# Matmul order in the wide products: all high-weight products of a slab first, then all low-weight ones

## The chip, the cores and the metric

The kernel runs on one core of a Trainium2 chip. The metric is the device time of one execution in microseconds (us), the median over runs. Lower is better.

## The reference

The reference is two blocks over 256 tokens of width 1024. The first is a gated mixer followed by a feed-forward of retrieved single-neuron experts, the second is two layers with two SwiGLU feed-forwards and an attention mixer each. What matters here are the feed-forwards:

```python
# first block: 16384 experts, 8 heads of 16 chosen ones per token
act = jax.nn.gelu(jnp.einsum('thkd,td->thk', expert_u[ib], hb), approximate=False)
return jnp.einsum('thk,thkd->td', gb * act, expert_v[ib])
...
# second block, four times, D_FF = 2816
def swiglu(h, w_gate, w_up, w_down):
    return (jax.nn.silu(h @ w_gate) * (h @ w_up)) @ w_down
```

The kernel computes the expert feed-forward densely: all 16384 experts for all tokens, with a matrix G of gates that is zero where an expert was not chosen. Everything is float32.

## The kernel before

**Slabs.** All weights come from one stream in HBM, cut into slabs of 128 by 1024 numbers (512 KB). A ring of four buffers (`RING = 4`) holds them: `raw` as it landed, `w_hi` (ACT casts it, line 714) and `w_lo` (DVE subtracts `w_hi` from `raw`, line 1192). Both parts are of the type fp32r. The activations are split in the same way into `h_hi` and `h_lo`, which lie side by side in `h_parts`. A product of two float32 numbers is thus taken as high times high, plus high weight times low activation, plus low weight times high activation. The product of the two low parts is left out.

**Two ways of multiplying a slab.** A slab is eight k-tiles of 128 rows (`KT = 8`) that are summed in one PSUM region. `three` (line 1989) issues three matmuls of 256 columns for each k-tile. `wide` (line 2011) issues two: the high weights against high and low activations at once (512 columns, a whole PSUM bank: high products in the left half, low ones in the right half), and then the low weights against the high activations (256 columns, added to the left half). The two halves are added later by ACT (lines 772 and 774) and DVE (lines 1276 and 1283).

**The loops.** `mlp` (line 2103) is the PE program of a feed-forward. For each step it calls `feed`, which multiplies the step's one slab (experts, `fronts_ == 1`) or two slabs (SwiGLU: gate and up, `fronts_ == 2`) into the tile `front`, and then `drain` of the step before, which multiplies the third slab with the hidden values of that step into the tile `acc`. In the expert loop `drain` is twelve matmuls of 512 columns, in the SwiGLU loops twenty-four of 256. The expert loop has 108 steps with a `feed` (20 more steps come with a `drain` alone, after them), each SwiGLU has 22 steps. `feed` uses `wide` for all 108 slabs of the expert loop, and in each SwiGLU from step 2 on for all slabs but the very last (39 slabs of 44).

**What orders the work.** Each engine has a program written out by hand, and semaphores between them. PE waits for `lo_ready` once ahead of a slab (`wait_slab`), and counts `slab_used` up once, on the last matmul of a slab. ACT and DVE take `front` after that count, and ACT may overwrite `w_hi` of that ring buffer after it. SP loads the next slab into a ring buffer when `lo_ready` says that `raw` was split.

Of the kernel before, what the change touches and what calls it, by code (L numbers as in the profile page):

```python
# [28 lines left out]
P = 128  # L29
T = 256  # L30
D = 1024
KT = D // P
# [15 lines left out]
RING = 4  # L48
# [144 lines left out]
def build(nc, stream, x_in, cols_in, ones_in, keys_in, wpool_in, mixc_in, attc_in, out):  # L193
# [5 lines left out]
    at = 0  # L199
# [51 lines left out]
    with ExitStack() as ctx:  # L251
# [7 lines left out]
        w_hi = sb("w_hi", W_HI, [RING, D], F32R)  # L259
        w_lo = sb("w_lo", W_LO, [RING, D], F32R)  # L260
        h_parts = sb("h_parts", H_HI, [2, KT, T], F32R)
        assert H_LO == H_HI + KT * T
        h_hi, h_lo = h_parts[:, 0, :, :], h_parts[:, 1, :, :]
# [116 lines left out]
        fronts = front[:, :, :]  # L380
# [1601 lines left out]
        def _(pe):  # L1982
            def mm(out, lhsT, rhs, start, stop, **kw):
                return nc.tensor.matmul(out, lhsT, rhs, start=start, stop=stop, **kw)  # L1984
# [23 lines left out]
                    r = readers[j - before]  # L2008
                    pe.wait_ge(tile_read[r], reads(r, j - before))

            def wide(bank, slot, k):

                c = k * P
                mm(bank, w_hi[:, slot, c:c + P], h_parts[:, :, k, :], k == 0, False, skip_group_check=True)
                return mm(bank[:, 0:T], w_lo[:, slot, c:c + P], h_hi[:, k, :], False, k == KT - 1,
                          skip_group_check=True)

            def project(name, i, n, hi, lo, lows=None, ks=range(KT), parts={}, sum_of=None):

# [83 lines left out]
            def mlp(n0, steps, fronts_, done, seeded, banks_done, q=None, more=0, late_sum=False):  # L2103
                per_step = fronts_ + 1

                def wait(turn, turns, sm, v):
                    if turn is None:
                        pe.wait_ge(sm, v)
                    else:
                        pe.wait_ge(sm, turn * turns + v)  # L2110

                def feed(s, n, turn=None, turns=0, sum_of=None):
                    S0 = done + s
                    whole = fronts_ == 1 or s >= 2
                    if s >= 2 or turn is not None:

                        wait(turn, turns, scaled_ready, S0 - 1 if fronts_ == 1 else S0)
                    if q is not None and s == 0:
                        first_two([fronts[:, 0, f * T:(f + 1) * T] for f in range(2)], n, q, True)
                        return  # L2120
                    for f in range(fronts_):
                        wait_slab(n + f, turn, turns * per_step)
                        at = f if whole and fronts_ == 2 else s % 2
                        alone = f == 1 and s == steps - 1 and turn is None
                        for k in range(KT):
                            if whole and not alone:
                                ins = wide(fronts[:, at, :], (n + f) % RING, k)
                                continue
                            ins = three(fronts[:, at, f * T:(f + 1) * T], (n + f) % RING, k * P,
                                        h_hi[:, k, :], h_lo[:, k, :], k == 0, k == KT - 1)  # L2130
                            if sum_of is not None and f == 0 and k == 3:
                                norm(sum_of)
                        ins.then_inc(slab_used, 1)

                def drain(s, n, turn=None, turns=0, last=False):

                    S0 = done + s
                    wait(turn, turns, mid_lo_ready, S0 + 1)
                    wait_slab(n, turn, turns * per_step)
                    begin = s == 0 and not seeded and turn is None  # L2140
                    for b in range(4 if seeded else 0):

                        a, c = [part[:, s % 2, b // 2 * P:(b // 2 + 1) * P] for part in (mid_hi, mid_lo)]
                        hi, lo = [part[:, n % RING, b % 2 * D // 2:(b % 2 + 1) * D // 2] for part in (w_hi, w_lo)]
                        mm(banks[:, b, :], a, hi, False, False, skip_group_check=True)
                        mm(banks[:, b, :], c, hi, False, False, skip_group_check=True)
                        ins = mm(banks[:, b, :], a, lo, False, False, skip_group_check=True)
                        if last:
                            ins.then_inc(bank_done, 1)
                    for m in range(0 if seeded else KT):  # L2150

                        ins = three(acc[:, m, :], n % RING, m * P, mid_hi[:, s % 2, :], mid_lo[:, s % 2, :],
                                    begin and m % 2 == 0, False, skip_group_check=True)
                        if last and m % 2:

                            ins.then_inc(bank_done, 1)
                    if not last:
                        ins.then_inc(slab_used, 1)
                    else:
                        pe.wait_ge(bank_done, banks_done + 4)  # L2160
                        pe.sem_inc(slab_used, 1)

                feed(0, n0)
                n = n0 + fronts_
                turns = 4 if fronts_ == 2 else 2

                if q is not None and not late_sum:
                    norm(q)
                feed(1, n, sum_of=q if late_sum else None)
                if q == 2:  # L2170

                    for tt in range(TT):
                        pe.wait_ge(token_diag_ready, tt + 1)
                        ins = mm(tile[:, 2, tt * P:(tt + 1) * P], ones, final_diag[:, tt, :], True, True)
                    ins.then_inc(token_spread, 1)
                drain(0, n + fronts_)
                n += per_step
                loops = (steps - 2 - (fronts_ == 2)) // turns
                with pe.Fori(0, loops) as turn:
                    for c in range(turns):  # L2180
                        feed(2 + c, n + c * per_step, turn, turns)
                        drain(1 + c, n + c * per_step + fronts_, turn, turns)
                for s in range(2 + loops * turns, steps):
                    m = n + (s - 2) * per_step
                    feed(s, m)
                    drain(s - 1, m + fronts_)
                for s in range(steps - 1, steps + more):
                    drain(s, n0 + steps * per_step - 1 + (s - steps + 1), last=s == steps + more - 1)
# [42 lines left out]
            n = first["w_in"]  # L2231
            for i in range(44):
                if i in (MIX_V, MIX_V + 2):
                    project_tokens("w_in", i, i - MIX_V, n + i, h_hi, h_lo)
                elif i < PLAIN:
                    free_tile(i)
                    pe.wait_ge(landed[i], 16)
                    for k in range(KT):
                        if i == 0:
                            pe.wait_ge(h0_by["dve" if k & 2 else "act"], k // 4 * 2 + k % 2 + 1)  # L2240
                        ins = mm(tile_buf(i), raw[:, i, k * P:(k + 1) * P], h0[:, k, :], k == 0, k == KT - 1)
# [9 lines left out]
                if i == FIRST_LEVEL + 18:  # L2251
# [3 lines left out]
                    for pair in range(HEADS // 2):  # L2255
                        ins = outputs(vv, pair, fr[:, pair, :],
                                      lambda h: (S[:, h % 2, h // 2, :], S_off[:, h % 2, h // 2, :],
                                                 S[:, 2 + h % 2, h // 2, :]))
                    ins.then_inc(o_done, 1)
                if i == FIRST_LEVEL + 20:  # L2260
                    pe.wait_ge(o_sq, 1)
                    pe.wait_ge(mixc_landed, 16)
                    for b in range(2):
                        ins = mm(banks[:, b, :], head_ones,
                                 osq[:, 2 * b:2 * b + 2, :].rearrange("p a t -> p (a t)"), True, True)
# [3 lines left out]
            n = first["branch"]  # L2269
            for m in range(8):  # L2270
# [3 lines left out]
                for half in range(2):  # L2274
                    for k in range(4):
                        kk_ = 4 * half + k
                        ins = three(tile_buf(j, half), (n + m) % RING, kk_ * P, y_hi[:, kk_, :],
                                    y_lo[:, kk_, :], k == 0, k == 3)
                ins.then_inc(slab_used, 1)
            n = first["w_out"]  # L2280
            for m in range(8):
                project("w_out", m, n + m, h_hi, h_lo)
            if "peer" in first:
# [29 lines left out]
                n = first["wquery"]  # L2313
# [27 lines left out]
                for a in range(TOPK):  # L2341
                    pe.wait_ge(chosen_ready, a + 1)
                    for side in range(2):
                        for tt in range(TT):
                            ins = mm(tile[:, side, tt * P:(tt + 1) * P],
                                     chosen[:, a % 8, (side * TT + tt) * HEADS:(side * TT + tt + 1) * HEADS, :]
                                     .rearrange("p h k -> p (h k)"), ident_16[:, :],
                                     a == 0 and side == 0 and tt == 0, a == TOPK - 1, skip_group_check=True)
                    ins.then_inc(chosen_used, 1)
                    if a == GATES_AT:  # L2350
                        pe.wait_ge(picks_ready, 1)
                        for tt in range(TT):
                            ins = nc.tensor.transpose(tile[:, 2, tt * P:(tt + 1) * P],
                                                      gts[:, tt, :, :].rearrange("p h k -> p (h k)"), ident)
# [31 lines left out]
                for tt in range(TT):  # L2386
                    pe.wait_ge(x_tokens_by_act, tt + 1)
                    for k in range(KT):
                        if k == KT // 2:
                            pe.wait_ge(x_tokens_by_dve, tt + 1)  # L2390
                            pe.wait_ge(token_squares, 1)
                        ins = nc.tensor.transpose(turned_x(k)[:, tt * P:(tt + 1) * P],
                                                  x_tokens[:, tt, k * P:(k + 1) * P], eye[:, :])
# [5 lines left out]
            for kind, i in layer_stages():  # L2399
# [5 lines left out]
                elif kind == "even":  # L2405
# [36 lines left out]
                    n = first["even_in"]  # L2442
# [21 lines left out]
                    for g in range(2):  # L2464
                        pe.wait_ge(stick_e, g + 1)
                        for pair in (2 * g, 2 * g + 1):
                            ins = outputs(av, pair, fr[:, pair, :],
                                          lambda h: [az[:, h, c * P:(c + 1) * P] for c in range(3)])
                        ins.then_inc(ao_done, 1)
                    n = first["even_out"]  # L2470
# [4 lines left out]
                else:  # L2475
# [40 lines left out]
                    n = first["qkv"]  # L2516
# [119 lines left out]
```

## Time and profile before

| | |
|---|---|
| median of 3 runs | 2080.64 us (2077.79 to 2083.43) |
| the profiled execution | 2078.67 us, its span 2076.9 us |
| PE matmul busy | 2021.4 us, 97% of the span, 13232 matmuls |
| PE weight loads busy | 1822.9 us, 88% |
| DVE busy | 1511.5 us, 73% |
| ACT busy | 1126.5 us, 54% |
| DMA | 353.71 MB, mean 170 GB/s |
| mean granted TensorE clock | 0.996 |
| chain that ended last | PE 88%, DVE 7%, ACT 3% |

The expert loop lies between 423 and 1085 us of the span, the four SwiGLU feed-forwards after it. Matmuls are pipelined: the time that the profile gives for one matmul is longer than the distance from its start to the start of the next, so durations of matmuls can't be added up. What can be added up are distances between starts, and the pieces of the chain that ended last.

### The profile page before, as it was taken

The numbers are of one execution on the slowest core, as the hardware profiler recorded it, in microseconds if no ns is written. First come the engines' busy times: TensorE is split into PE (matmuls) and PEld (weight loads), VectorE is DVE, ScalarE is ACT, GpSimd is POOL, SyncE is SP. The second block draws the span as 40 slices with busy tenths as digits, with TensorE's granted clock in tenths as the row PEclk, the third lists the DMA queues.
The fourth block names the chain that finished last, engine by engine and source line by source line (L and its number), as shares of the span: only waits on it lengthen the run. The fifth ranks groups of instructions, "written<-read, shape, count | busy, mean of one in ns | idle before, by whom it ended". The sixth has DMA issues, their size and how long they took to land.

```text
span 2076.9 us, 37250 instructions
## 1 busy us (share of the span) xinstructions
PE 2021.4 (97%) x13232; PEld 1822.9 (88%) x13232; DVE 1511.5 (73%) x2563; ACT 1126.5 (54%) x1834; POOL 59.8 (3%) x40
## 2 busy tenths in 40 slices
PE   7999899999999999999999999999999999999998
PEld 7999888978888888888888999899999999999998
DVE  5868898867777777777777667666667667957665
ACT  5444528855555555555555555645555555645554
POOL 0000530000000000000000000000000000000000
PEclk9999999999999999999999999999999999999999
DMA  6346542146556555555664555445555555535553
GB/s 216 127 135 214 181 130 82 44 162 187 187 184 190 191 182 190 188 188 185 205 228 164 185 188 167 137 158 182 182 183 183 182 182 183 163 123 173 186 187 112
DMA packets 101464, 353.71 MB, mean 170 GB/s; under 512 B 11392, under 2 KB 16640, under 8 KB 101120
## 3 DMA queue, kind: packets, MB, share of 16 engines
q1 hardware_dynamic: 100944, 350.13, 52.0%
q10 hardware_dynamic: 432, 2.36, 0.3%
q8 instruction: 61, 1.00, 0.2%
q14 instruction: 27, 0.22, 0.0%
HBM read 348.77 MB, written 3.67 MB: 170 GB/s over the span
## 4 chain that ended last, share of the span: by engine, by line
PE 88%; DVE 7%; ACT 3%; issue 1%; DMA 0%; SPq 0%; DVEq 0%; ACTq 0%
PE front L1984 39%; PE acc L1984 33%; PE tile L1984 15%; DVE w_lo L1192 1%; ACT w_hi L714 1%; DVE chosen L1709 0%; DVE cand L1652 0%; ACT G L962 0%; PE front L2501 0%; DMA raw<-stream 0%; DVE x L1372 0%; ACT picks_raw L956 0%; ACT picks_mid L956 0%; DVE rstd L1214 0%; ACT h_parts L740 0%
## 5 line engine op out<-in xcount | busy, mean ns | idle before, releaser
L1984 PE MATMUL front<-h_parts,w_hi 128*128 128x512 f32 (+1 forms) x2432 | 813.7, 384 | 5.0 <-ACT h_parts L740 2.1
L1192 DVE TENSOR_TENSOR w_lo<-raw,w_hi 128x1024 fp32r<-128x1024 f32 x612 | 748.4, 1223 | 90.5 <-ACT w_hi L714 90.0
L714 ACT CAST w_hi<-raw 128x1024 fp32r<-128x1024 f32 x628 | 656.2, 1046 | 143.4 <-PE tile L1984 67.4
L1984 PE MATMUL front<-h_parts,w_lo 128*128 128x256 f32 x2272 | 636.2, 281 | 0.0
L1984 PEld LDWEIGHTS front<-h_parts,w_hi 128*128 128x128 f32 x2432 | 448.0, 189 | 100.3 <-issue 3.9
L1984 PEld LDWEIGHTS front<-h_parts,w_lo 128*128 128x128 f32 x2272 | 430.2, 189 | 4.1
L1984 PE MATMUL tile<-h_parts,w_hi 128*128 128x256 f32 x1344 | 248.0, 286 | 5.7 <-DVE w_lo L1192 2.6
L1276 DVE TENSOR_TENSOR scaled<-front,scaled 128x512 f32<-128x512 f32 x76 | 52.6, 692 | 228.4 <-ACT scaled L774 228.4
L1984 PEld LDWEIGHTS tile<-h_parts,w_hi 128*128 128x128 f32 x1344 | 209.3, 192 | 8.9 <-issue 6.9
L1984 PE MATMUL acc<-w_hi,mid_hi 128*128 128x512 f32 x512 | 203.1, 397 | 3.4 <-DVE mid_lo L1300 3.4
L1984 PE MATMUL acc<-mid_hi,w_hi 128*128 128x256 f32 x704 | 199.3, 283 | 2.5 <-DVE mid_lo L1337 2.5
L1984 PE MATMUL acc<-w_lo,mid_hi 128*128 128x512 f32 x512 | 201.1, 393 | 0.0
L778 ACT ACTIVATE scaled<-scaled 128x256 f32<-128x256 f32 x188 | 78.9, 420 | 223.6 <-DVE scaled L1279 119.9
L1984 PE MATMUL acc<-w_hi,mid_lo 128*128 128x512 f32 x512 | 199.9, 390 | 0.0
L1984 PE MATMUL acc<-mid_lo,w_hi 128*128 128x256 f32 x704 | 199.3, 283 | 0.0
L1984 PE MATMUL acc<-mid_hi,w_lo 128*128 128x256 f32 x704 | 199.3, 283 | 0.0
L1984 PE MATMUL tile<-h_parts,w_lo 128*128 128x256 f32 x672 | 188.6, 283 | 0.0
L1984 PEld LDWEIGHTS acc<-mid_hi,w_hi 128*128 128x128 f32 x704 | 133.7, 190 | 6.4 <-DVE mid_lo L1337 2.9
L772 ACT COPY scaled<-front 128x256 f32<-128x256 f32 x108 | 40.5, 375 | 179.2 <-PE front L1984 179.2
L1984 PEld LDWEIGHTS acc<-mid_hi,w_lo 128*128 128x128 f32 x704 | 134.0, 190 | 0.0
L1984 PEld LDWEIGHTS acc<-mid_lo,w_hi 128*128 128x128 f32 x704 | 133.9, 190 | 0.0
L1984 PEld LDWEIGHTS tile<-h_parts,w_lo 128*128 128x128 f32 x672 | 128.7, 191 | 0.0
(324 smaller groups left out, 2525.2 us busy)
## 6 DMA issues: line engine op xcount, KB each, us to landing
raw<-stream SPq DMA_DIRECT2D x632, 512.0 KB, 3.8
early_u<-stream SPq DMA_DIRECT2D x20, 512.0 KB, 3.6
early_activations<-early_out SPq DMA_DIRECT2D x20, 128.0 KB, 3.5
scaled<-early_activations SPq DMA_DIRECT2D x10, 128.0 KB, 3.9
x<-x_t SPq DMA_DIRECT2D x2, 512.0 KB, 4.8
keysT<-keys_t ACTq DMA_DIRECT2D x1, 1024.0 KB, 6.5
attc<-attention_constants ACTq DMA_DIRECT2D x1, 1024.0 KB, 6.0
out_t<-h SPq DMA_DIRECT2D x4, 256.0 KB, 2.5
```

Source lines behind the costliest of these rows:

```text
L714: nc.scalar.copy(w_hi[:, s, :], raw[:, s, :]).then_inc(hi_ready, 1)
L772: nc.scalar.copy(scaled[:, k, 0:T], fronts[:, k, T:2 * T]).then_inc(lows_out, 1)
L778: nc.scalar.activation(scaled[:, k, 0:T], scaled[:, k, 0:T], func).then_inc(gate_ready, 1)
L1192: nc.vector.tensor_tensor(w_lo[:, s, :], raw[:, s, :], w_hi[:, s, :].bitcast(F32), ALU.subtract).then_inc(lo_ready, 1)
L1276: nc.vector.tensor_tensor(to, fronts[:, :, 0:T], to, ALU.add).then_inc(parts_added, 1)
L1984: return nc.tensor.matmul(out, lhsT, rhs, start=start, stop=stop, **kw)
```

## The change

Within a slab the eight products of the high weights (512 columns each) are issued first, and then the eight of the low weights (256 columns each), where they alternated before. The same sixteen matmuls are issued, on the same operands, and `slab_used` is counted up on the same last matmul.

```diff
-            def wide(bank, slot, k):
-
-                c = k * P
-                mm(bank, w_hi[:, slot, c:c + P], h_parts[:, :, k, :], k == 0, False, skip_group_check=True)
-                return mm(bank[:, 0:T], w_lo[:, slot, c:c + P], h_hi[:, k, :], False, k == KT - 1,
-                          skip_group_check=True)
+            def wide(bank, slot):
+
+                for k in range(KT):
+                    mm(bank, w_hi[:, slot, k * P:(k + 1) * P], h_parts[:, :, k, :], k == 0, False,
+                       skip_group_check=True)
+                for k in range(KT):
+                    ins = mm(bank[:, 0:T], w_lo[:, slot, k * P:(k + 1) * P], h_hi[:, k, :], False, k == KT - 1,
+                             skip_group_check=True)
+                return ins
...
-                        for k in range(KT):
-                            if whole and not alone:
-                                ins = wide(fronts[:, at, :], (n + f) % RING, k)
-                                continue
+                        if whole and not alone:
+                            ins = wide(fronts[:, at, :], (n + f) % RING)
+                        for k in range(0 if whole and not alone else KT):
                             ins = three(fronts[:, at, f * T:(f + 1) * T], (n + f) % RING, k * P,
                                         h_hi[:, k, :], h_lo[:, k, :], k == 0, k == KT - 1)
```

## Rows read from the trace of the kernel before

**Rows 1.** The profile's page, its part on the chain that ended last.
```profile
PE 88%; DVE 7%; ACT 3%; issue 1%; DMA 0%; SPq 0%; DVEq 0%; ACTq 0%
```

**Rows 2.** Busy time by window: window and its length, PE, PEld, DVE, ACT, POOL, clock, DMA.
```profile
600.00:1020.00 420.00, 420.00 (x2104) 352.92 (x2104) 314.07 (x451) 224.87 (x376) 0.00 (x0) 1.00 0.60 189
1190.00:1290.00 100.00, 99.49 (x675) 91.69 (x674) 68.10 (x93) 54.60 (x78) 2.04 (x2) 1.00 0.58 189
```

**Rows 3.** Groups of PE by line and shape: count, busy us, mean ns, idle before.
```profile
L1984 PE MATMUL front<-h_parts,w_hi 128*128 128x512 f32 x2112 | 753.9, 398 | 2.7 <-ACT G L962 1.4 <-DVE scaled L1279 1.2
```

**Rows 4.** The chain in order of time, expert loop: start us, us, what.
```profile
701.12 2.78 PE acc L1984 x12
703.90 2.81 PE front L1984 x16
706.71 2.78 PE acc L1984 x12
```

**Rows 5.** The chain in order of time, first SwiGLU.
```profile
1202.83 2.87 PE acc L1984 x24
1205.70 5.65 PE front L1984 x32
1211.35 2.88 PE acc L1984 x24
```

**Rows 6.** The chain in order of time, projections of 256 columns, end of the expert loop.
```profile
143.41 74.49 PE tile L1984 x624
...
1029.98 54.73 PE acc L1984 x240
```

**Rows 7.** Timeline of PE, end of the expert loop: eight 512-column steps.
```profile
1040.10 0.39 PE L1984 MATMUL acc<-w_lo,mid_hi 128*128 128x512 f32 x1
...
1041.91 0.39 PE L1984 MATMUL acc<-w_hi,mid_lo 128*128 128x512 f32 x1
```

**Rows 8.** Timeline, expert loop: a drain behind a wide slab, first, second and ninth matmul.
```profile
700.96 0.40 PE L1984 MATMUL acc<-w_hi,mid_hi 128*128 128x512 f32 x1
...
701.20 0.40 PE L1984 MATMUL acc<-w_hi,mid_lo 128*128 128x512 f32 x1
...
702.82 0.40 PE L1984 MATMUL acc<-w_lo,mid_hi 128*128 128x512 f32 x1
```

**Rows 9.** Timeline, SwiGLU: three alternating pairs, from one low product to the fourth.
```profile
1206.13 0.28 PE L1984 MATMUL front<-h_parts,w_lo 128*128 128x256 f32 x1
1206.25 0.40 PE L1984 MATMUL front<-h_parts,w_hi 128*128 128x512 f32 x1
1206.49 0.28 PE L1984 MATMUL front<-h_parts,w_lo 128*128 128x256 f32 x1
1206.60 0.40 PE L1984 MATMUL front<-h_parts,w_hi 128*128 128x512 f32 x1
1206.83 0.28 PE L1984 MATMUL front<-h_parts,w_lo 128*128 128x256 f32 x1
1206.95 0.40 PE L1984 MATMUL front<-h_parts,w_hi 128*128 128x512 f32 x1
1207.19 0.28 PE L1984 MATMUL front<-h_parts,w_lo 128*128 128x256 f32 x1
```

**Rows 10.** Timeline, expert loop: the step from a drain into a wide slab.
```profile
703.74 0.39 PE L1984 MATMUL front<-h_parts,w_hi 128*128 128x512 f32 x1
703.97 0.28 PE L1984 MATMUL front<-h_parts,w_lo 128*128 128x256 f32 x1
704.08 0.40 PE L1984 MATMUL front<-h_parts,w_hi 128*128 128x512 f32 x1
...
705.02 0.42 DVE L1300 TENSOR_TENSOR mid_lo<-hid,mid_hi 128x256 fp32r<-128x256 f32 x1
...
706.55 0.40 PE L1984 MATMUL acc<-w_hi,mid_hi 128*128 128x512 f32 x1
```

## The prediction

> **What bounds the kernel.** I read the page's chain first: 88% of it is PE [rows 1], so a nanosecond taken from or given to a matmul in the feed-forwards should reach the end. The busy times by window say the same for the two stages that the change touches: in the expert loop PE is busy 420.00 of 420.00 us, in a SwiGLU 99.49 of 100.00, while DVE has 314.07 of 420 and 68.10 of 100, the DMA engines 60% and 58%, and the granted clock is 1.00 in both, the upper level of 2.4 GHz [rows 2]. The reader is to see there that PE waits for nobody. It issues matmuls back to back, and the only question is the distance from one start to the next. That distance isn't the profile's duration of a matmul (398 ns for the 512-column ones of `wide`, rows 3): those overlap. It is read from pieces of the chain and from starts in the timeline.
>
> **How often.** The 512-column products of `wide` are 2112 [rows 3]; by eight that is 264 slabs: 108 in the expert loop, and 4 times 39 = 156 in the SwiGLUs. The change reorders inside these alone. It adds and removes no matmul, no weight load, no wait and no count of a semaphore, and moves no DMA. A weight load goes with each matmul before and after, 16 in a slab. So the price is one difference: sixteen matmuls alternating against eight and eight.
>
> **Alternating, as it is.** In the expert loop the sixteen take 2.81 us [rows 4], or 351 ns for a pair. In a SwiGLU thirty-two take 5.65 us, that is 2.825 us for a slab and 353 ns for a pair [rows 5]. Single starts show where it goes: three pairs take 1207.19 - 1206.13 = 1.06 us. Of these the distances behind a 256-column matmul are 0.12, 0.11 and 0.12, mean 117 ns, and those behind a 512-column one 0.24, 0.23 and 0.24, mean 237 ns [rows 9].
>
> **Runs of one width.** 256 columns: 2.88 us for 24 is 120.0 ns [rows 5], and 74.49 us for 624 is 119.4 ns [rows 6]. So a low product in a run costs some 3 ns more than between wide ones. 512 columns: here the trace has two prices. In a long run the distance is 1041.91 - 1040.10 = 1.81 us for eight, 226 ns [rows 7]; over all 240 it is 228.0 ns [rows 6]. But in a drain that follows alternating products the first eight take 702.82 - 700.96 = 1.86 us, 232.5 ns each, the first of them 240 [rows 8]. It takes about ten matmuls until the short distance is reached. So a run of 512s behind 256s begins at the dear price, and a run of 512s behind 512s is cheap at once.
>
> **Expert loop.** The eight high products follow the twelve 512-column matmuls of a drain, whose last ones are already at the short distance; the first one of `front` behind it keeps it, 703.97 - 703.74 = 0.23 us, and the first pair takes 0.34 where later ones take 0.35 to 0.36 [rows 10]. I take 227 ns (between the 226 of rows 7 and the 228 of rows 6) and 120 ns: 8 x 227 + 8 x 120 = 2776 ns against 2810. That is 34 ns less for a slab, and 108 x 34 = 3.7 us. The drain behind it starts from 256-column matmuls, as it does now from alternating ones; I leave it at 2.78 us.
>
> **SwiGLU.** Here what goes before the eight high products is always a run of 256s: the 24 of a drain, or the eight low products of the slab before. The nearest row is the drain behind a wide slab, so 1.86 us for the eight; with 8 x 120 = 0.96 that is 2.82 us against 2.825. The gain is 5 ns for a slab, and 156 x 5 = 0.8 us.
>
> **What hides nothing.** Were PE shorter by 1%, the others would have to keep up. In the expert loop DVE finishes `mid_lo` at 705.02 + 0.42 = 705.44 and the drain that reads it starts at 706.55 [rows 10]: 1.1 us to spare, thirty times the gain of a slab. DVE and DMA have 25% and 40% to spare [rows 2]. `slab_used` falls at the end of a slab as before, so nothing that ACT or DVE do is triggered at another point.
>
> **The sum.** -3.7 - 0.8 = -4.5 us. Against the profiled execution, 2078.67 us (the span of 2076.9 and 1.8 around it), it would be 2074.2; that execution lies 2.0 us under the median of the three runs, 2080.64. Against the median it is 2076.1.
>
> **The bounds.** Low end: the slow start isn't there in a SwiGLU and its 512s cost 227 as well, 1816 + 960 = 2776 ns against 2825, 156 x 49 = 7.6 us, with the 3.7 together -11.3, 2069.3. Were also the 256s in the groups at the 117 of the alternation, another 2112 x 3 = 6.3 us would go: 2063.0. High end: the 512s stay at 237 and the 256s rise from 117 to 120. Then a pair costs 357 against 351 and 353: 864 x 6 + 1248 x 4 = 10.2 us, 2090.8.
>
> **The rivals.** *Both loops gain.* The dear start of rows 8 belongs to what alternates ahead of it, not to 256s as such, and a pure run of 256s leaves no such debt. Then the SwiGLUs give 7.6 us too: 2069.3. For it speaks that the start in rows 8 follows an alternation; against it that the first 512 of a SwiGLU slab behind a drain of pure 256s is no faster than others (the 32 take 5.65, twice 2.825, with no cheap beginning, where the expert loop has 2.81).
>
> *Order means nothing.* What a matmul costs would depend on its width alone, and the small differences between the rows on what surrounds them: 2080.6. With the run prices, 232 (2.78 us by 12, rows 4) and 120, the slab costs 8 x 352 = 2816 against 2810 and 2825: 108 x 6 - 156 x 9 = -0.8 us, 2079.9. For it speaks that these prices hit the alternating pair within 1 ns; against it the 226 of rows 7. By the Trainium skill's "TensorE: Matmul & The Clock Gate", section "Back-to-back issue gap", a warm matmul takes columns by 2.4 and 2.5 ns more, whatever stands beside it, so 215.8 and 109.2 ns and no difference by order. The trace has 226 to 237 and 117 to 120 in their places, and 512s differ by what went before, so the rule misses what is at stake here.
>
> *Low products in a run are held up by their weight loads.* This is the case on the other side. A low product between wide ones follows a load that had a whole 512-column stream to hide under; in a group each load has only a 256-column stream. The place is the eight low products, the price is the 3 ns from 117 to 120 [rows 5, 9], and with it goes nothing back if the 512s keep their 237 because that is the price of a moving operand in two halves (`h_parts`), which no drain has. Then +10.2 us, 2090.8. If the 512s fall half way, to 233, the pair is 353 and nothing is lost: that is the point from which it decides, 512s above 233 ns. For it speaks that loads are the same number in a smaller cover; against it that `front`'s first 512 behind a drain takes 0.23 with the same operand [rows 10]. The same page's part "LDWEIGHTS (loading the stationary operand)" puts a load of 128 columns at P by 1.2, some 107 ns, which is just the 256-column stream and half the 512-column one. By that rule the groups would be the worse order; no row here shows a load alone.
>
> **How the numbers follow.** My forecast has a chance of 0.42, both loops gain 0.22, order means nothing 0.22, the slower case 0.14. A measurement of this kernel tells about 0.3%, 6.2 us, from no change. Faster by more than that is the second case nearly whole and a part of the first, whose 4.5 us lie near the line: 0.33. Slower is most of the last case: 0.12. The rest, 0.55, is within. The range goes from 2068, which holds the case of both loops, to 2086, which cuts the dear end of the slower case; it leaves out about 2 in 10.
>
> **What would show it.** In the chain by time a `front` piece of 16 in the expert loop should be 2.78 where it was 2.81, one of 32 in a SwiGLU 5.64 where it was 5.65, and the drains 2.78 and 2.88 as before. In the timeline the high products of an expert slab should start 0.22 to 0.23 apart, those of a SwiGLU slab 0.24 falling to 0.23, and the low products 0.12 everywhere. A drain piece of 12 longer than 2.78, 512s above 233 ns, or any idle time of PE in the loops would prove me wrong. So would a `front` piece of 32 at 5.56, on the better side.

## The result and the profile after

The changed kernel takes 2066.15 us (median of 4 runs, 2063.86 to 2067.55), the kernel before 2080.5: a ratio of 0.993 with an interval of 0.9912 to 0.9947, or 14.4 us less. I had forecast 2076.1 with a range from 2068 to 2086. The sign was right, the size was a third of what came, and the time lies under the range. The profiled execution took 2066.98 us (span 2065.2), 11.7 less than that of before.

Of the busy times only PE's moved by more than 5 us (2021.4 to 2010.3). The page's first part, and then busy time by window in the two loops, in the columns of [rows 2]:

```profile
PE 2010.3 (97%) x13232; PEld 1827.6 (88%) x13232; DVE 1511.1 (73%) x2563; ACT 1123.6 (54%) x1834; POOL 59.8 (3%) x40
```
```profile
600.00:1015.00 415.00, 415.00 (x2111) 354.61 (x2111) 314.66 (x452) 224.51 (x376) 0.00 (x0) 1.00 0.60 192
1190.00:1275.00 85.00, 85.00 (x572) 78.63 (x571) 57.09 (x75) 44.87 (x63) 0.00 (x0) 1.00 0.57 186
```

PE is busy all the time in both windows, at the same granted clock, and DVE has as much work as before. The gain is in the distances of matmuls. The chain in order of time shows it by pieces, for the expert loop (answering to [rows 4]) and for the first SwiGLU (answering to [rows 5]):

```profile
699.96 2.75 PE acc L1984 x12
702.71 2.77 PE front L1984 x16
...
1191.39 5.59 PE front L1984 x32
1196.98 2.88 PE acc L1984 x24
1199.86 5.59 PE front L1984 x32
```

The `front` piece of 16 went from 2.81 to 2.77, the two slabs of a SwiGLU from 5.65 to 5.59, the drain of a SwiGLU stayed at 2.88. And the drain of the expert loop, of which the change touches no line, went from 2.78 to 2.75. In nanoseconds (medians of the distances between starts, over 106 steps of the expert loop and 18 of the first SwiGLU) these are 2810 to 2766, 5648 to 5587, 2879 to 2880 and 2783 to 2747. The sum is

- 108 x 44 = 4.8 us for the expert slabs,
- 108 x 36 = 3.9 us for the expert drains,
- 78 x 61 = 4.8 us for the SwiGLU slabs,

together 13.5 us. The profiled execution shows 11.7, and one reason is that it comes 2.6 us later to the loops than the one of before did (its first product of `front` with `w_hi` starts at 425.9, in the one of before at 423.3), over instructions in which the kernels are the same:

```profile
L1984 PE MATMUL front<-h_parts,w_hi x2432: 278/389/628, 425.9 to 2047.5; 128*128 128x512 f32 x163, 128*128 128x256 f32 x25
```

The granted clock of the 300 us from 20 to 320 was 0.99 in this execution and 1.00 in the other. From that first product to the end of the span the difference is 14.3 us, 0.8 more than the sum. By stages it is 8.4 in the expert loop, 0.5 in the first SwiGLU (granted clock 0.99 there, 1.00 before), 2.4 in the second and third, 1.4 in the last, and 1.4 in the stretch ahead of the last, where the order wasn't changed (clock 1.00, 0.99 before). So single executions differ by a microsecond or two with the clock at the borders of stages, and only the pieces inside the loops repeat to the nanosecond.

The timeline shows the sixteen matmuls of a slab in the expert loop, and the drain ahead of them:

```profile
699.80 0.40 PE L1984 MATMUL acc<-w_hi,mid_hi 128*128 128x512 f32 x1
700.03 0.40 PE L1984 MATMUL acc<-w_hi,mid_lo 128*128 128x512 f32 x1
700.26 0.39 PE L1984 MATMUL acc<-w_lo,mid_hi 128*128 128x512 f32 x1
700.49 0.40 PE L1984 MATMUL acc<-w_hi,mid_hi 128*128 128x512 f32 x1
700.73 0.39 PE L1984 MATMUL acc<-w_hi,mid_lo 128*128 128x512 f32 x1
700.96 0.39 PE L1984 MATMUL acc<-w_lo,mid_hi 128*128 128x512 f32 x1
...
702.54 1.98 PE L1984 MATMUL front<-h_parts,w_hi 128*128 128x512 f32 x8
704.36 1.11 PE L1984 MATMUL front<-h_parts,w_lo 128*128 128x256 f32 x8
705.31 0.40 PE L1984 MATMUL acc<-w_hi,mid_hi 128*128 128x512 f32 x1
```

The reader is to see three prices. The eight high products take 704.36 - 702.54 = 1.82 us, 227 ns each. The eight low ones take 0.95: the first 113 ns, the second 119, the rest 120. And the drain behind them starts dear, but less so and for a shorter time than before: 233, 236, 228, 232, 231, and then 227 to its end, where before it was 241, 237, 233, 236, 224, 231, 236, 228, 233, 231 until it came to 227 ([rows 8] show the first of them and the mean of the first eight).

### The profile page after: what moved, and what is told of

Same layout as the page of the kernel before. It is cut to its first block, busy times and chain, and to the rows that moved or that the text cites. A ratio compares the mean times of both kernels' runs of the same rounds, so it can differ in the third digit from the quotient of the medians.

```text
span 2065.2 us, 37250 instructions
## 1 busy us (share of the span) xinstructions
PE 2010.3 (97%) x13232; PEld 1827.6 (88%) x13232; DVE 1511.1 (73%) x2563; ACT 1123.6 (54%) x1834; POOL 59.8 (3%) x40
## 4 chain that ended last, share of the span: by engine, by line
PE 89%; DVE 6%; ACT 3%; issue 1%; DMA 0%; ACTq 0%; SPq 0%; DVEq 0%
PE front L1984 39%; PE acc L1984 34%; PE tile L1984 16%; DVE w_lo L1192 1%; ACT w_hi L714 1%; DVE chosen L1709 0%; DVE cand L1652 0%; DMA raw<-stream 0%; ACT G L962 0%; PE front L2503 0%; ACT picks_raw L956 0%; ACT picks_mid L956 0%; DVE rstd L1214 0%; ACT h_parts L740 0%; DVE rest L1621 0%
## 5 line engine op out<-in xcount | busy, mean ns | idle before, releaser
L1984 PE MATMUL front<-h_parts,w_hi 128*128 128x512 f32 (+1 forms) x2432 | 587.4, 378 | 3.6 <-ACT h_parts L740 1.7
L1984 PEld LDWEIGHTS front<-h_parts,w_hi 128*128 128x128 f32 x2432 | 437.6, 189 | 79.1 <-issue 2.4
L1984 PEld LDWEIGHTS front<-h_parts,w_lo 128*128 128x128 f32 x2272 | 319.2, 191 | 20.7
L1984 PE MATMUL front<-h_parts,w_lo 128*128 128x256 f32 x2272 | 337.5, 282 | 0.0
```

## The experiments

All are edits of `wide`. Where it helps, `high(k)` stands for the 512-column product of k-tile k and `low(k)` for its 256-column product. Where a kernel was executed only once, its time says little (single executions of the kernel before lie between 2077.8 and 2083.4 us), and the pieces of the chain decide.

**The new order in one kind of loop only.**

```diff
-            def wide(bank, slot):
+            def wide(bank, slot, size):
...
+                for k0 in range(0, KT, size):
+                    for k in range(k0, k0 + size):
+                        high(k, k == 0, False)
+                    for k in range(k0, k0 + size):
+                        ins = low(k, False, k == KT - 1)
...
-                            ins = wide(fronts[:, at, :], (n + f) % RING)
+                            ins = wide(fronts[:, at, :], (n + f) % RING, KT if fronts_ == 1 else 1)
```

> The new order in the expert loop alone; the SwiGLUs alternate as before. Theory 'widths': a 512-column matmul costs 227 ns in a run and more only in the first five behind 256-column ones, and alternation makes this worse. The drain gets its 36 ns from the order of the feed ahead of it: expert pieces 2.77 and 2.75 (before 2.81 and 2.78), SwiGLU pieces 5.65 and 2.88 as before, and the time falls by 108 x (44 + 36) ns = 8.7 us, to about 2072. Rival 'whole program': the drain's gain comes from something common to the run (layout of the program, clock), so that pieces of both loops move alike, whichever is reordered.

Measured: 2074.09 us (6 runs), ratio 0.9966 (0.9954 to 0.9979), 6.5 us less where 8.7 was expected; the interval holds both. The chain by time, expert loop and then first SwiGLU:

```profile
704.63 2.75 PE acc L1984 x12
707.37 2.77 PE front L1984 x16
...
1233.31 5.65 PE front L1984 x32
1238.96 2.88 PE acc L1984 x24
```

> The new order in the SwiGLUs alone. Theory 'widths': SwiGLU feed 5.59 and drain 2.88, expert loop 2.81 and 2.78 as before, time less by 156 x 30.5 ns = 4.8 us, to about 2076. With the other kernel's 8.7 this makes 13.5. Rival 'whole program': the expert drain is 2.75 here too.

Measured (`fronts_ == 2` in the same edit): 2076.71 us (10 runs), ratio 0.9982 (0.9973 to 0.9992), 3.9 us less where 4.8 was expected; here too the interval holds both.

```profile
703.23 2.81 PE front L1984 x16
706.04 2.78 PE acc L1984 x12
...
1235.37 2.88 PE acc L1984 x24
1238.24 5.59 PE front L1984 x32
```

Each loop moves alone, to the nanosecond as in the changed kernel. The drain's 36 ns come from the order of the feed ahead of it in the same loop: the rival "whole program" is out. The two gains add to 10.4 us, and the intervals of the three ratios allow the 13.5 of the trace for the whole.

**Is it where the low product writes?**

```diff
                 for k0 in range(0, KT, 1):
...
-                    return mm(bank[:, 0:T], w_lo[:, slot, k * P:(k + 1) * P], h_hi[:, k, :], start, stop, ...)
+                    return mm(bank[:, T:2 * T], w_lo[:, slot, k * P:(k + 1) * P], h_hi[:, k, :], start, stop, ...)
```

> Alternating order as before, but the low products are added to the right half of the bank, which the halves' sum makes the same result. Theory 'widths': nothing changes, 2.81 and 5.65, drain 2.78, 2080. Rival 'bank': what costs in the alternation is that a 256-column product is added onto columns that the 512-column one ahead has only begun to write; here its columns are written last by the one ahead and first touched again 256 columns later, so the distances would move by several ns: 2.77 or less if that was the cost, or above 2.81 if the new place is worse.

Measured: 2080.54 us, beside 2080.59 for the kernel before. The pieces are those of before, and so is each single distance in the expert loop (227, 113, 233, 117, 241, 120, 236, ...).

```profile
705.36 2.81 PE front L1984 x16
708.17 2.78 PE acc L1984 x12
```

In the alternating order it doesn't matter which columns the low product writes, or how soon they are written again.

**Is it the two arrays of weights, or the two widths?** The alternating order, with low products of 512 columns (the product of the low parts is added to the sum, which the other kernels leave out):

```diff
-                    return mm(bank[:, 0:T], w_lo[:, slot, k * P:(k + 1) * P], h_hi[:, k, :], start, stop, ...)
+                    return mm(bank, w_lo[:, slot, k * P:(k + 1) * P], h_parts[:, :, k, :], start, stop, ...)
```

> Alternating order, but the low products have 512 columns too (low weights against high and low activations, so the product of the low parts is added). Theory 'widths': with one width the alternation of weight arrays is free: 16 x 227 = 3.63 us for a slab in the expert loop, 7.26 plus some 0.03 for two in a SwiGLU, drain 2.72, and about 2081 + 108 x 0.82 + 156 x 0.80 - 6 = 2288 us. Rival 'arrays': taking weights in turn from the two arrays costs: 237 ns for each, 3.79 us for a slab, about 2330 us.

Measured: 2286.42 us against 2288 expected. All sixteen distances of an expert slab are 227 ns, and all twelve of the drain too:

```profile
702.00 2.72 PE acc L1984 x12
704.73 3.63 PE front L1984 x16
708.35 2.72 PE acc L1984 x12
...
1286.26 7.28 PE front L1984 x32
1293.54 2.87 PE acc L1984 x24
```

This settles what the alternation costs: not that weights come in turn from `w_hi` and `w_lo`, but that widths change. With one width in the whole expert loop there is no dear start anywhere. In the SwiGLU, where the 512s stand behind a drain of 256s, they start 233, 236, 228, 232, 231 and go on at 227. That is 28 ns on top for the run (the sum of what is above 226.7), once, whether eight 512s follow as in the changed kernel or thirty-two as here.

**Smaller groups.** Four high and four low products, twice in a slab; and two and two, four times:

```diff
-                for k0 in range(0, KT, 8):
+                for k0 in range(0, KT, 4):      # and 2
```

> Four high products, four low ones, twice in a slab. In the trace of the changed kernel the 512s behind 256s start 233, 236, 228, 233, 231 and then 227 ns apart, and the first 256s behind 512s 113, 119, then 120. Theory 'each change of width has its own price': the same start at each change. Expert feed 4x227 + 472 + 930 + 472 = 2781 ns (2.78), SwiGLU pair of slabs 4 x 1402 = 5608 (5.61), expert drain 2.75. Rival 'debt': what a change costs grows with how few of a kind stand together, as in the alternation (expert drain 2.78 behind it): then the drain is above 2.75 here and the feed above 2.78.

> Two and two, four times in a slab. 'Each change has its own price': expert feed 453 + 232 + 3 x 701 = 2788 (2.79), SwiGLU 8 x 701 = 5608 (5.61), drain 2.75; the two 256s take 113 and 119. Rival 'debt': like the alternation, towards 2.81, 5.65 and a drain of 2.78.

Measured: 2072.03 us with four and 2064.14 with two. The chain by time with four:

```profile
704.72 2.77 PE acc L1984 x12
707.49 2.78 PE front L1984 x16
```

and with two, in a second execution of it (timed below):

```profile
704.77 2.73 PE acc L1984 x12
707.50 2.77 PE front L1984 x16
...
1237.92 2.88 PE acc L1984 x24
1240.80 5.57 PE front L1984 x32
```

Neither theory holds. The feed with four came as "each change has its own price" said (2780 ns against 2781, 5614 against 5608), but its drain is 2767 and not 2747. With two, feed and drain are both cheaper than that theory allows: 2777 against 2788, 5574 against 5608, drain 2730 against 2750. So there is no debt that grows as groups shrink, and no fixed price for a change either. What the drain has on top of its 2720 (twelve times 226.7) is 63 ns behind single products, 10 behind twos, 47 behind fours and 28 behind eights.

**How far back does it reach?** Only the last pair of k-tiles grouped, or only the last k-tile alternating:

```diff
+                for k in range(KT - 2):          # last_pair
+                    high(k, k == 0, False)
+                    low(k, False, False)
+                for k in (KT - 2, KT - 1):
+                    high(k, False, False)
+                for k in (KT - 2, KT - 1):
+                    ins = low(k, False, k == KT - 1)
...
+                for k in range(KT - 1):          # single_behind
+                    high(k, k == 0, False)
+                for k in range(KT - 1):
+                    low(k, False, False)
+                high(KT - 1, False, False)
+                ins = low(KT - 1, False, True)
```

> The first six k-tiles alternate, only the last two are grouped (two high, two low). What decides how dear the start of the 512s behind them is? Theory 'what stands directly ahead': the last two low products alone, so the expert drain is 2.73 as behind groups of two, while the feed stays near 2.81. Rival 'debt of the slab': the alternation ahead of them counts, and the drain stays at 2.77 to 2.78.

> Seven high products, seven low ones, and then the last k-tile's high and low product. 'Directly ahead': the drain follows a single low product, as in the alternation, and is at 2.77 to 2.78; feed 7 x 227 + 832 + 233 + 115 = 2767 (2.77). Rival 'debt of the slab': a slab nearly all grouped leaves a drain of 2.75.

Measured: 2073.65 us and 2075.27 (one execution each). The chain by time of the first, and then of the second:

```profile
704.09 2.81 PE front L1984 x16
706.89 2.75 PE acc L1984 x12
```
```profile
704.18 2.77 PE front L1984 x16
706.95 2.78 PE acc L1984 x12
```

Behind seven and seven, one alternating k-tile brings the drain back to 2783 ns, with the very distances of the kernel before (241, 237, 233, 236, ...). Behind six alternating k-tiles, one group of two brings it to 2747, the distances of the changed kernel. The debt of the slab is out: changing the last one or two k-tiles is enough to move the drain all the way. But the 2.73 expected for `last_pair` didn't come: behind four such groups the drain was 2730, behind one it is 2747. So the last two low products alone don't settle it, and how far back it reaches stays open.

**What makes a run of 256s take 120 ns?** The new order, with low products of 64 instead of 128 weight columns (their term is left out for half of the output features), and with low products that stream 128 instead of 256 columns (left out for half of the tokens):

```diff
-                    return mm(bank[:, 0:T], w_lo[:, slot, k * P:(k + 1) * P], h_hi[:, k, :], start, stop, ...)
+                    return mm(bank[0:P // 2, 0:T], w_lo[:, slot, k * P:k * P + P // 2], h_hi[:, k, :], start, stop, ...)
...
+                    return mm(bank[:, 0:P], w_lo[:, slot, k * P:(k + 1) * P], h_hi[:, k, 0:P], start, stop, ...)
```

> The new order, but each low product has only 64 of its 128 weight columns, so that its weight load is half as long while its stream of 256 columns and the number of instructions stay; the low term of half the output features is left out. Theory 'load': a 256 in a run takes 120 and not 113 ns because the next load, begun with it, doesn't fit under it. Then the low products fall to 113: expert feed 2.72, and the 512s of the drain behind them lose their dear start, 2.72. Rival 'issue': 120 ns is what two instructions take to be issued, whatever they carry, and all stays at 2.77 and 2.75.

> The new order, but each low product streams only 128 of the 256 columns; the low term of half the tokens is left out. 'Load' and 'issue' alike: 120 ns is a floor for a matmul with a whole weight load of its own, so a low product in a run stays at about 120 and the feed at 2.77. Rival 'columns': the distance goes with the columns (0.44 ns each and some 7 on top), 64 ns, feed 2.32, and about 2066 - 264 x 0.45 = 1948 us.

Measured: 2058.33 us with half the weight columns and 2057.14 with half the streamed columns. The chain by time, half the weight columns first:

```profile
703.99 2.74 PE acc L1984 x12
706.73 2.73 PE front L1984 x16
```
```profile
703.80 2.66 PE front L1984 x16
706.46 2.83 PE acc L1984 x12
```

With half the load the low products fall from 120 to 113 ns (the first two take 118 and 117), with the number of instructions unchanged: what two instructions take to be issued isn't what makes it 120, the load is part of it. (Half the weight columns are also half the rows written; the two weren't told apart.) 113 is half of the 227 that twice the columns take, so the distance seems to be the stream's alone; that is an inference. But the drain behind stays at 2747 with its 233, 236, 228: that part of the "load" theory fell. With half the stream and the whole load the first low product takes 57 ns, which is half of 113, but all the others still take 110 to 115. "Columns" (1948 us) is far out, and a floor is there, at some 112 rather than the 120 I had said. The Trainium skill's "TensorE: Matmul & The Clock Gate", section "LDWEIGHTS (loading the stationary operand)", takes the nanoseconds of a load as its columns divided by 1.2, for 128 columns an estimated 107; the floor of 112 ns measured here is near it.

No kernel of this series had both the short stream and the short load, but the trace of the kernel before has rows elsewhere that tell the load from the issue of two instructions. First four bf16 matmuls of 128 columns with their four loads, then 32 plain fp32 ones (those of the loops are fp32r) that stream only 2 columns, each with a load of 128:

```profile
304.11 0.23 PEld L1984 LDWEIGHTS tile<-ident,chosen 128*128 128x128 bf16 x4 [1.52 <-DVE chosen L1709]
304.11 0.40 PE L1984 MATMUL tile<-ident,chosen 128*128 128x128 bf16 x4 [1.12 <-DVE chosen L1709]
...
2065.41 3.75 PEld L1984 LDWEIGHTS tile<-lane,sq 128*128 128x128 f32 x32 [0.32 <-issue]
2065.44 3.81 PE L1984 MATMUL tile<-lane,sq 128*128 128x2 f32 x32
```

The four bf16 ones start 66, 56 and 55 ns apart, so a load and a matmul can be issued every 56 ns. The 32 others start 112 ns apart (median), with hardly a stream at all. The floor at 112 ns is thus not what two instructions take to be issued, whatever they carry; what is left is the load of 128 columns of 4-byte numbers. That last step is by exclusion. The price of the floor shows behind the low products too: the drain starts at 292 ns and takes 2832, so that half of the low columns saved only 26 ns of a step of 5513.

**Two versions meant to be better.** In a SwiGLU, low products first in the gate slab and high products first in the up slab, so that a step has one change from 256 to 512 columns:

```diff
+                if low_ahead:
+                    for k in range(KT):
+                        low(k, k == 0, False)
+                for k in range(KT):
+                    ins = high(k, k == 0 and not low_ahead, k == KT - 1 and low_ahead)
+                if not low_ahead:
+                    for k in range(KT):
+                        ins = low(k, False, k == KT - 1)
...
+                            ins = wide(fronts[:, at, :], (n + f) % RING, fronts_ == 2 and f == 0)
```

> In a SwiGLU the gate slab issues its low products first, behind the drain's 256s, and its high ones last, in front of the up slab's high ones, so that a step has one change from 256 to 512 columns where it had two. 'Each start of a run of 512s costs 28 ns': 960 + 1841 + 1813 + 952 = 5566 against 5587, 78 x 21 ns = 1.6 us less than the changed kernel, about 2064.5; expert loop as there. Rival: a run of 512s behind 512s of another slab starts dear as well, 5.59.

> Groups of two again, now timed against the kernel before. By the trace of the first look: expert feed 2777 and drain 2730 against 2810 and 2783, two SwiGLU slabs 5574 against 5648: 108 x 86 + 78 x 74 = 15.1 us less, about 2065.5, and 1.6 us less than the changed kernel by the same sum (108 x 6 + 78 x 13). Rival: the single look at 2064.1 was chance and the whole is no faster than 2068.

Measured: 2066.28 us and a ratio of 0.9936 (0.9922 to 0.9949) for the first, 2067.43 us and 0.9941 (0.9927 to 0.9954) for the groups of two. The chain by time of the first, in a SwiGLU:

```profile
1238.18 2.88 PE acc L1984 x24
1241.06 5.57 PE front L1984 x32
```

Its piece came as worked out (5567 ns against 5566): the second eight 512s, behind the first eight, cost 227 from the start. In groups of two the pieces repeated those of the first execution. But 1.6 us are 0.08% of the time, and the three kernels can't be told apart by their runs (0.993, 0.9936 and 0.9941 with intervals of 0.003). Neither beats the changed kernel by its times, though their pieces are shorter, and the 2064.1 of the first execution was chance.

## Why the prediction fell short

**What bounds the kernel, and how often: right.** PE was busy for 415.00 of 415 us in the expert loop, and what was taken from a distance reached the end. Inside the two windows PE waited for no other engine and for no DMA.

**Expert slab: right, slightly short.** I said 2776 ns and it is 2766. The high products cost 227 as said. The low ones cost 120 in a run, but the first two of a run only 113 and 119, which my 8 x 120 left out: 8 ns, and rounding is the rest. Together 108 x 10 = 1.1 us.

**Expert drain: the first step that failed.** "The drain behind it starts from 256-column matmuls, as it does now from alternating ones; I leave it at 2.78 us." It went to 2747 ns, and this is 3.9 us. I had taken "behind a 256" as the condition of the dear start, when the row showed "behind an alternation". `single_behind` and the changed kernel differ in the last k-tile's order, and their drains by exactly these 36 ns.

**SwiGLU slab: the second, by the same error.** "The nearest row is the drain behind a wide slab, so 1.86 us for the eight." Behind a run of 256s the eight take 1841 ns where I had 1860, and the low ones 952 where I had 960; a slab is 2793 and not 2820. Against the 5 ns forecast the gain is 30.5, and 156 x 25.5 = 4.0 us; some 19 ns of each slab belong to the start of the 512s and 8 to the first two low products. `low_512` shows the same start behind a drain of 256s, with nothing alternating in widths anywhere near.

4.5 forecast, and 1.1 + 3.9 + 4.0 more, make the 13.5 of the trace.

**The rivals.** "Both loops gain" had the mechanism right in part ("The dear start of rows 8 belongs to what alternates ahead of it"), with a chance of 0.22. But it let the dear start vanish, which it doesn't (28 ns stay), and still left the drain at 2.78. It gave -11.3 and named no consequence for the drain; that is why the range ended at 2068. The low bound of 2063.0 that I had worked out, and then left out of the range, lay below the result, but by another sum: it has the dear start gone and the low products at 117 ns, where they rose to 119, and nothing for the drain. Had the range held the result by it, that would have been luck. "Order means nothing" is out: the same sixteen matmuls take 2766, 2770, 2777, 2780, 2806 or 2810 ns by order alone. The Trainium skill's "TensorE: Matmul & The Clock Gate", section "Back-to-back issue gap", gives 2.5 ns on top of the columns for a matmul by itself, and for a stream of loads and matmuls about 131 ns at 512 columns; I had left out that the first is for one by itself. Neither fits the distances here: 227 and 120 ns are 13 above 512 and 256 columns at the granted 2.4 GHz. The slower case had its place right, the low products rose from 117 to some 119, but the 512s fell to 227 in the expert loop and 230 on average in the SwiGLUs, under the 233 at which it would have begun to lose.

**The signs that I named.** The expert drain should have stayed at 2.78 and went to 2.75. The `front` pieces came to 2.77 and 5.59 where I had 2.78 and 5.64, and the one that "would prove me wrong", a piece of 32 near 5.56, was nearer than mine.

**What stays open** is why a change of width costs what it does. The distances repeat to the nanosecond from step to step, and they depend on the order of the last few matmuls in a way (63, 10, 47 and 28 ns behind ones, twos, fours and eights) that none of my theories gives. What is shown is what it isn't: the columns written (`low_right`), the array of the weights (`low_512`), a debt gathered over the slab (`single_behind`, `last_pair`), or the length of the loads ahead of the drain (`low_half_load`).

## What to carry to other kernels

Where PE is the bound and matmuls of two widths share a loop, put those of one width together, and look at the matmuls behind them too: 3.9 of the 13.5 us here fell to a group that wasn't touched. Groups needn't be large: in twos a step of the expert loop took 5507 ns, in eights 5513. When a price is read off a row, carry the whole neighbourhood of the row with it; a run behind a single narrow product isn't a run behind a run of narrow ones. And when one reading is used in two places, work out what both lose if it is wrong, before the range is narrowed.

## What the runs showed of the hardware

- At a granted clock of 1.00, fp32r matmuls with a weight load each start 226.7 ns apart at 512 columns in a run, in whatever order their weights come from two arrays (`low_512`), and 120 ns apart at 256.
- In a run, a 256-column product takes 120 ns with a load of 128 columns, 113 with one of 64 (`low_half_load`). A 128-column stream with a load of 128 takes about 112 (`low_128`), and a 2-column plain fp32 one in the kernel before as well. So a stream of 256 and a load of 128 are each near 113, and both together take 120.
- A load and a matmul can be issued 56 ns apart (bf16, 128 columns, in the kernel before), so that the 112 ns aren't the issue of two instructions.
- A run of 512s behind a run of 256s takes 233, 236, 228, 233, 231 before it reaches 227, 28 ns in all; behind an alternation it is 63 ns over ten matmuls, behind twos 10 ns and behind fours 47. It is the same whether the 256s had short or whole loads (`low_half_load`).
